# Spreading per-token values over the partitions of a one-core Trainium2 convolution layer: split columns against a rounded identity

## The reference

```
hn = x * rsqrt(mean(x*x) + eps) * norm_g                 # per token
a, b, gate = split(hn @ w_in, 3)                         # w_in 1024 x 3072
u  = a * sigmoid(b)
u  = causal depthwise conv of u, 31 taps, + conv_b
u  = (u - mean(u)) * rsqrt(var(u) + eps) * ln_g + ln_b   # per token
y  = x + (silu(u) * silu(gate)) @ w_out                  # w_out 1024 x 1024
```

## Time and profile before

| | |
|---|---|
| median of 3 runs | 356.37 us (356.23 to 356.69) |
| the profiled execution | 356.49 us, span 354.7 us |
| granted TensorE clock | 1.00 over the whole span |
| PE (matmul) | 349.1 us busy, 98% |
| PEld (weight load) | 288.6 us, 81% |
| DVE (VectorE) | 323.1 us, 91% |
| ACT (ScalarE) | 232.2 us, 65% |
| POOL (GpSimd) | 270.2 us, 76% |
| chain that ended last | PE 82%, DVE 8%, issue 3%, DMA 2% |

### The profile page before, as it was taken

The page is one execution under the profiler, slowest core; times in us unless marked ns, Lnnn a source line. Parts: engine busy times, 40 slices in busy tenths (PEclk is TensorE's granted clock), DMA queues, the critical chain, the costliest instruction groups (busy, mean ns, idle before and its releaser), DMA issues.

```text
span 354.7 us, 4758 instructions
## 1 busy us (share of the span) xinstructions
PE 349.1 (98%) x1564; PEld 288.6 (81%) x1564; DVE 323.1 (91%) x514; ACT 232.2 (65%) x334; POOL 270.2 (76%) x194
## 2 busy tenths in 40 slices
PE   8999999999999999999999999999999999999996
PEld 7878888888888888888888888888788877888886
DVE  4779799999999999989999998997699999999972
ACT  6899684667936870998659777976774872443400
POOL 0129999999999998789999999885698551359240
DMA  7995011211410321404120411341733497046152
GB/s 255 404 412 225 33 61 59 71 50 59 118 61 10 91 80 59 118 2 118 59 60 6 115 59 31 99 109 61 234 121 119 138 416 276 2 136 219 63 206 90
DMA packets 30520, 43.51 MB, mean 123 GB/s; under 512 B 18336, under 2 KB 18848, under 8 KB 30496
## 3 DMA queue, kind: packets, MB, share of 16 engines
q1 hardware_dynamic: 30352, 43.21, 36.7%
q10 hardware_dynamic: 144, 0.00, 0.0%
HBM read 34.82 MB, written 4.19 MB: 110 GB/s over the span
## 4 chain that ended last, share of the span: by engine, by line
PE 82%; DVE 8%; issue 3%; DMA 2%; SPq 2%; ACT 2%; DVEq 0%; ACTq 0%
PE mm L634 63%; PE acc L713 9%; PE mm L713 8%; DMA sgate<-x 2%; DVE nat L1207 2%; DVE x_lo L1243 2%; PE mm L651 2%; SPq L496 1%; DVE sgate L1236 1%; DVE nat L1228 1%; ACT mm L939 1%; DVE sgate L1263 1%; DVE nat L1275 0%; SPq L522 0%; ACT sgate L775 0%
## 5 line engine op out<-in xcount | busy, mean ns | idle before, releaser
L634 PE MATMUL mm<-x_hi,w_hi 128*128 128x512 f32 x352 | 137.4, 390 | 0.0
L634 PE MATMUL mm<-x_hi,w_lo 128*128 128x512 f32 x352 | 137.0, 389 | 0.0
L634 PE MATMUL mm<-x_lo,w_hi 128*128 128x512 f32 x352 | 136.9, 389 | 0.0
L1187 DVE SCALAR_TENSOR_TENSOR acc<-u,chan,acc 128x512 f32<-128x512 f32 x157 | 110.4, 747 | 0.1
L1496 POOL TENSOR_TENSOR pconv<-pconv,prod 128x512 f32<-128x512 f32 x60 | 78.2, 1344 | 1.3 <-ACT prod L870 1.3
L634 PEld LDWEIGHTS mm<-x_hi,w_hi 128*128 128x128 f32 x352 | 66.1, 188 | 13.6
L634 PEld LDWEIGHTS mm<-x_hi,w_lo 128*128 128x128 f32 x352 | 66.1, 188 | 13.7
L634 PEld LDWEIGHTS mm<-x_lo,w_hi 128*128 128x128 f32 x352 | 66.1, 188 | 13.6
L1187 DVE SCALAR_TENSOR_TENSOR acc<-u,w_sum,acc 128x512 f32<-128x512 f32 x90 | 67.2, 746 | 2.4 <-ACT acc L852 2.3
L870 ACT ACTIVATE prod<-u,chan 128x512 f32<-128x512 f32 x69 | 48.0, 716 | 19.9 <-POOL pconv L1496 18.4
L1440 POOL TENSOR_TENSOR w_lo<-raw,w_hi 128x1024 fp32r<-128x1024 f32 (+1 forms) x21 | 50.2, 2390 | 8.8 <-ACT w_hi L819 8.8
(11 more groups left out here) (109 smaller groups left out, 536.2 us busy)
## 6 DMA issues: line engine op xcount, KB each, us to landing
raw<-w_in SPq DMA_DIRECT2D x22, 512.0 KB, 3.4
nat<-x_t SPq DMA_DIRECT2D x16, 256.0 KB, 6.2
sgate<-x SPq DMA_DIRECT2D x8, 512.0 KB, 10.2
raw<-w_out SPq DMA_DIRECT2D x8, 512.0 KB, 3.3
nat<-x SPq DMA_DIRECT2D x8, 512.0 KB, 6.8
y<-nat SPq DMA_DIRECT2D x15, 256.0 KB, 2.2
raw_late<-w_out SPq DMA_DIRECT2D x4, 512.0 KB, 3.8
sig<-w_out SPq DMA_DIRECT2D x4, 512.0 KB, 4.3
```

The costliest lines, as they stand in the source:

```text
L634: ins = nc.tensor.matmul(bank(("unit", m, h)), w[:, m % 3, k, :], xx[:, k, half(h)], start=(k == 0 and i == 0), stop=(k == KC - 1 and i == 2))
L1187: ins = nc.vector.scalar_tensor_tensor(dst, chain_in(j, chain, k), tap(j, chain, k), chain_bank(j, chain), ALU.mult, ALU.add)
```

## The change

All six spreads are done in one way. A column of four per-token values is split into a rounded high part and a rounded low part (fp32r, four numbers per partition each). For each tile, TensorE takes the high column, broadcast to 128 columns, as the stationary operand against a rounded identity of 128 columns, and then the low column in the same way, accumulated. That is 8 fp32r matmuls of 128 columns for each spread, with 8 weight loads. The diagonals of VectorE and of ScalarE and the rounded ones go; a rounded identity is made once by VectorE. The two parts of rms and of the mean are made by VectorE (for rms in `split_rms`, for half 1 ahead of `split_raw(0, 5)` and for half 0 behind the last `make_hn` of half 1; for the mean at the end of `moments`), those of rstd by GpSimd behind the power in `inverse_deviation`. Buffers in SBUF are moved a little.

```diff
-DIAGS_BEFORE = {4: (4, 5, 6), 5: (7,)}
+SPLIT_RMS_BEFORE = 5
...
+            def spread_columns(spread, hi, lo, h):
+                for i in range(TPH):
+                    t = TPH * h + i
+                    nc.tensor.matmul(spread[:, i * P:(i + 1) * P], hi[:, t:t + 1].to_broadcast([P, P]), ident_r[:],
+                                     start=True, stop=False)
+                    ins = nc.tensor.matmul(spread[:, i * P:(i + 1) * P], lo[:, t:t + 1].to_broadcast([P, P]), ident_r[:],
+                                           start=False, stop=True)
+                return ins
             def spread_rms(h):
                 if h == 1:
-                    spread = rms_spread(1).rearrange("p (t q) -> p t q", t=TPH)
-                    pe.wait_ge(ones_r_ready, 1)
-                    pe.wait_ge(diag_hi_ready, TPH)
-                    nc.tensor.matmul(spread, ones_r[:], diags[:, 0, :, :], start=True, stop=False)
-                    pe.wait_ge(diag_lo_ready, TPH)
-                    ins = nc.tensor.matmul(spread, ones_r[:], diags[:, 1, :, :], start=False, stop=True)
-                else:
-                    for i in range(TPH):
-                        pe.wait_ge(diag_ready, i + 1)
-                        ins = nc.tensor.matmul(rms_spread(0)[:, i * P:(i + 1) * P], ones[:], diag(i), start=True, stop=True)
-                ins.then_inc(rms_all_ready, 1)
+                    pe.wait_ge(ident_r_ready, 1)
+                pe.wait_ge(rms_lo_ready, NH - h)
+                spread_columns(rms_spread(h), rms_hi, rms_lo, h).then_inc(rms_all_ready, 1)
...
             def spread_mean(h):
-                pe.wait_ge(mv_ready, TPH * (h + 1))
-                for i in range(TPH):
-                    ins = nc.tensor.matmul(norm_spread(h, 0)[:, i * P:(i + 1) * P],
-                                           mean_var[:, TPH * h + i, 0:1].to_broadcast([P, P]), ident[:],
-                                           start=True, stop=True)
-                ins.then_inc(mean_spread, 1)
+                pe.wait_ge(mean_lo_ready, h + 1)
+                spread_columns(norm_spread(h, 0), mean_hi, mean_lo, h).then_inc(mean_spread, 1)
             def spread_rstd(h):
                 pe.wait_ge(rstd_ready, h + 1)
-                for i in range(TPH):
-                    t = TPH * h + i
-                    ins = nc.tensor.matmul(norm_spread(h, 1)[:, i * P:(i + 1) * P],
-                                           rstd[:, t:t + 1].to_broadcast([P, P]), ident[:], start=True, stop=True)
-                ins.then_inc(rstd_spread, 1)
+                spread_columns(norm_spread(h, 1), rstd_hi, rstd_lo, h).then_inc(rstd_spread, 1)
...
-            for t in range(TPH):
-                rms_diagonal(t)
...
-            nc.vector.tensor_scalar(ones_r[:], ones[:], 1.0, None, ALU.mult).then_inc(ones_r_ready, 1)
+            def split_rms(h):
+                dve.wait_ge(rms_ready, rms_count(TPH * (h + 1) - 1))
+                nc.vector.tensor_scalar(rms_hi[:, tiles_of(h)], rms[:, tiles_of(h)], 1.0, None,
+                                        ALU.mult).then_inc(rms_hi_ready, 1)
+                dve.wait_ge(rms_hi_ready, NH - h)
+                nc.vector.tensor_tensor(rms_lo[:, tiles_of(h)], rms[:, tiles_of(h)], rms_hi[:, tiles_of(h)].bitcast(F32),
+                                        ALU.subtract).then_inc(rms_lo_ready, 1)
...
+                dve.wait_ge(mv_ready, TPH * (h + 1))
+                nc.vector.tensor_scalar(mean_hi[:, tiles_of(h)], means, 1.0, None, ALU.mult).then_inc(mean_hi_ready, 1)
+                dve.wait_ge(mean_hi_ready, h + 1)
+                nc.vector.tensor_tensor(mean_lo[:, tiles_of(h)], means, mean_hi[:, tiles_of(h)].bitcast(F32),
+                                        ALU.subtract).then_inc(mean_lo_ready, 1)
...
-                for t in DIAGS_BEFORE.get(k, ()):
-                    rms_diagonal(t)
+                if k == SPLIT_RMS_BEFORE - 1:
+                    dve.wait_ge(ident_in, 16)
+                    nc.vector.tensor_scalar(ident_r[:], ident[:], 1.0, None, ALU.mult).then_inc(ident_r_ready, 1)
+                if k == SPLIT_RMS_BEFORE:
+                    split_rms(1)
...
+            split_rms(0)
...
-                                        ALU.pow).then_inc(rstd_ready, 1)
+                                        ALU.pow).then_inc(rstd_pow, 1)
+                pool.wait_ge(rstd_pow, h + 1)
+                nc.gpsimd.tensor_scalar(rstd_hi[:, part], rstd[:, part], 1.0, None, ALU.mult).then_inc(rstd_hi_ready, 1)
+                pool.wait_ge(rstd_hi_ready, h + 1)
+                nc.gpsimd.tensor_tensor(rstd_lo[:, part], rstd[:, part], rstd_hi[:, part].bitcast(F32),
+                                        ALU.subtract).then_inc(rstd_ready, 1)
```

More of the change, by code:

```diff
@@ L164, in gated_conv_layer @@
         sig = sb("sig", [P, 2, HALF])
-        sb("gap_before_w", [P, 96])
+        ident_r = sb("ident_r", [P, P], F32R)
+        rms_hi = sb("rms_hi", [P, NT], F32R)
+        rms_lo = sb("rms_lo", [P, NT], F32R)
+        mean_hi = sb("mean_hi", [P, NT], F32R)
+        mean_lo = sb("mean_lo", [P, NT], F32R)
+        rstd_hi = sb("rstd_hi", [P, NT], F32R)
+        rstd_lo = sb("rstd_lo", [P, NT], F32R)
+        sb("gap_before_w", [P, 48])
         first = ExitStack()
@@ L177, in gated_conv_layer @@
             pconv = sb("pconv", [P, 2, HALF], F32, first)
-            ones_r = sb("ones_r", [P, P], F32R, first)
-            diags = sb("diags", [P, 2, TPH, P], F32R, first)
         wb = {}
@@ L200, in gated_conv_layer @@
         ones_ready = sem("ones_ready")
-        ones_r_ready = sem("ones_r_ready")
-        diag_ready = sem("diag_ready")
-        diag_hi_ready = sem("diag_hi_ready")
-        diag_lo_ready = sem("diag_lo_ready")
+        ident_r_ready = sem("ident_r_ready")
+        rms_hi_ready = sem("rms_hi_ready")
+        rms_lo_ready = sem("rms_lo_ready")
+        mean_hi_ready = sem("mean_hi_ready")
+        mean_lo_ready = sem("mean_lo_ready")
+        rstd_hi_ready = sem("rstd_hi_ready")
         rms_all_ready = sem("rms_all_ready")
@@ L241, in gated_conv_layer @@
         veps_ready = sem("veps_ready")
+        rstd_pow = sem("rstd_pow")
         rstd_ready = sem("rstd_ready")
@@ L460, in half, with tiles_of @@
             return slice(h * HALF, (h + 1) * HALF)
-        def diag(i):
-            return sgate[:, i, 0:P]
+        def tiles_of(h):
+            return slice(TPH * h, TPH * (h + 1))
         def words(columns):
@@ L789, in split_first @@
                                      raw[:, m, first_columns(part)], ACT.Copy).then_inc(w_first_hi, 1)
-            def rms_diagonal(t):
-                act.wait_ge(ident_in, 16)
-                act.wait_ge(rms_ready, rms_count(t))
-                nc.scalar.activation(diag(t), ident[:], ACT.Copy, scale=rms[:, t:t + 1]).then_inc(diag_ready, 1)
             def copy_rms(h):
@@ L1075, in _ @@
             nc.vector.memset(ones[:], 1.0).then_inc(ones_ready, 1)
-            dve.wait_ge(ones_ready, 1)
-            nc.vector.tensor_scalar(ones_r[:], ones[:], 1.0, None, ALU.mult).then_inc(ones_r_ready, 1)
             nc.vector.memset(half_neg[:], -0.5).then_inc(exponent_ready, 1)
@@ L1081, in _ @@
             dve.wait_ge(pads_ready, 2)
-            def rms_diagonal(t):
-                dve.wait_ge(ident_in, 16)
-                dve.wait_ge(rms_ready, rms_count(t))
-                i = t - TPH
-                nc.vector.tensor_scalar(diags[:, 0, i, :], ident[:], rms[:, t:t + 1], None,
-                                        ALU.mult).then_inc(diag_hi_ready, 1)
-                dve.wait_ge(diag_hi_ready, i + 1)
-                nc.vector.scalar_tensor_tensor(diags[:, 1, i, :], ident[:], rms[:, t:t + 1],
-                                               diags[:, 0, i, :].bitcast(F32), ALU.mult,
-                                               ALU.subtract).then_inc(diag_lo_ready, 1)
+            def split_rms(h):
[5 more added lines that the diff above has]
+                                        ALU.subtract).then_inc(rms_lo_ready, 1)
             def make_hn(h, k):
@@ L1202, in moments @@
                                       stats[:, t, :, :].rearrange("p g s -> p (g s)")).then_inc(mv_ready, 1)
+                means = mean_var[:, tiles_of(h), 0]
+                dve.wait_ge(mv_ready, TPH * (h + 1))
[3 more added lines that the diff above has]
+                                        ALU.subtract).then_inc(mean_lo_ready, 1)
             def centre(k, h):
```

## The result

The changed kernel takes 359.21 us (median of 4 runs, 359.09 to 359.34) against 356.47 us of the kernel before on the same chip (4 runs, 356.23 to 356.69): ratio 1.0077, 95% interval 1.006 to 1.0094. It is slower by 2.7 us; forecast were 1.1. The profiled execution grew from 356.49 to 359.21 us, its span from 354.7 to 357.1. So 2.4 us of the growth lie inside the span, and 0.3 outside it, between the span and the measured time.

What follows compares the result with a forecast made beforehand. TensorE alone bounds 36.94 to 254.58 us; afterwards VectorE's addition at 293.48 sets the end. The terms -0.03 (head) + 1.16 (rstd pairs on GpSimd) gave +1.1 us, 356.37 to 357.5 us, whole range 356.5 to 360.3 us.

Steps and rivals of the forecast that it cites:

- likeliest case: Whole kernel: the prediction's own sum, +1.1 us to 357.5 us, with its own range 356.9 to 358.4 us, chance 0.60.
- wide price of a narrow matmul: Rival on TensorE: a narrow matmul costs as much as a wide one, 0.227 us; +3.8 us, 360.2 us, chance 0.15.
- The price of a new spread: TensorE, each spread: 8 narrow matmuls at their weight loads' pace, 0.113 us each, 0.90 us a spread.
- rms(1), -0.03 us: Head, spread of rms(1): longer matmuls cost +0.45 us, TensorE's wait of 0.48 us goes; sum -0.03 us.
- rms(0), "Nothing": Spread of rms(0): 0.90 for 0.91 us on TensorE, VectorE's pair inside its idle 2.85 us; no change.
- Mean, 0.40 us a half: VectorE, end of `moments`: two dependent small instructions, 0.40 us a half, 0.80 in all; `centre` about 0.6 us later.
- rstd, 1.16 us on GpSimd: GpSimd behind the power: two instructions, 0.58 us a half; first scale, ScalarE's second SiLU and VectorE's gate 1.16 us later.
- "From 263.92 to 293.48 [...] nothing gives it back": VectorE up to TensorE's last wait: it waits only for ScalarE, which waits for it, so the 1.16 us stay.
- wait of 1.5 us for rstd(0): TensorE: its wait for rstd(0), about 0.93 us, grows by 0.58 to about 1.5 us, taken up by later waits.
- rivals of the matmul's price: TensorE, a narrow matmul at 0.227 us (360.2 us, chance 0.15) or 0.066 us (near 357.0 us, chance 0.08).

Runs made afterwards that it cites:

- e7: Changed kernel with all six spreads as float32 matmuls of the broadcast column, no splits or diagonals: 356.69 us, 1.0006 of the kernel before.
- e9: Changed kernel with rms two words apart and a third VectorE instruction copying rms into PSUM for the rms(0) subtract: 358.48 us, 1.0052 of the kernel before.
- e10: Changed kernel with the rms(0) split made by GpSimd right behind its power, none on VectorE: 358.24 us, 1.0046 of the kernel before.
- e3: Changed kernel with rms(0) spread by float32 matmuls of the broadcast column, without a split: 358.29 us, 1.0056 of the kernel before.
- e1: Changed kernel with the mean's subtract reading a copy of the high part in PSUM: 359.14 us, 1.0081 of the kernel before.
- e2: Changed kernel with the mean's spreads as in the kernel before, float32 without a split: 359.35 us, 1.0083 of the kernel before.
- e5: Changed kernel with rms(0) and both means spread in float32, leaving rms(1) and GpSimd's rstd pairs: 358.45 us, 1.0054 of the kernel before.
- e4: Changed kernel with the rstd spreads as in the kernel before, GpSimd without its pairs: 358.32 us, 1.006 of the kernel before.
- e6: Changed kernel with rms(0) and both rstd spread in float32, leaving rms(1) and the mean's split: 357.19 us, 1.0016 of the kernel before.
- e12: Changed kernel with GpSimd making the rms(0) pair, and its weight subtracts, deviations and scales reordered at 254 us: 358.51 us, 1.0058 of the kernel before.

## Why the prediction was off

The direction was right, and 359.21 lies in the whole range, but outside the 356.9 to 358.4 us of the likeliest case. That the whole range holds it is luck: the range reached so far only for the rival with the wide price of a narrow matmul, and that mechanism fell. Step by step:

- *The price of a new spread*: right. Narrow matmuls are 0.11 us apart, a spread 0.9 us, but for rstd(0) at the lower clock (0.21 and 1.6 us, which reached nothing). e7 adds that float32 spreads cost the same.
- *rms(1), -0.03 us*: right within what can be read; the wait at 23.26 went, and the pair took 0.16 and 0.17 us.
- *rms(0), "Nothing"*: wrong, and this is the step that failed. It took the pair as two short instructions inside VectorE's wait of 2.85 us. The wait ends only when the spread is there, which now needs the pair, so it covers a pair only up to a little over 1 us (e9's three instructions took 1.13 and cost nothing); and the pair was 1.96 us long in place of 0.35, as it had to stand for GpSimd's x_lo group (0.74 and 1.19 us). Price: 1.04 us at the restart of VectorE, carried whole to 254 us. e9 and e10 brought the restart back, and each took 0.7 us off the median span.
- *Mean, 0.40 us a half*: wrong in size for half 0, 2.5 us, by the same mechanism (and by a race that VectorE lost by 0.01 us). `centre` was 3.9 us late (1.04 of it from rms(0)) in place of 0.6. TensorE stood 1.48 us, and its granted clock fell afterwards (it didn't in e3, where it stood 1.58 us): the windows of the changed kernel (busy us of each engine, then the clock, third from last) show 0.74 in 256 to 262 us.

```profile
250.00:256.00 6.00, 5.68 (x26) 4.36 (x24) 3.47 (x10) 4.82 (x8) 3.68 (x2) 1.00 0.66 196
256.00:262.00 6.00, 4.84 (x23) 4.43 (x24) 5.90 (x16) 3.58 (x5) 5.31 (x10) 0.74 0.60 215
```

  None of this reached the end: e1 and e2 undo it, and the time stays.
- *rstd, 1.16 us on GpSimd*: right in size, 1.20 us from first weight subtract to last pair. The way it was to take was only half right. ScalarE's second SiLU does come later, and VectorE stands for it where nothing else has made it late (1.04 us in e5, 0.47 in e10); but in the changed kernel VectorE was late by itself and never stood there. What carries the 1.16 us in every kernel with the pairs is GpSimd's own queue, up to its last pair of scales. In e9 and e10, 1.5 us apart in VectorE's arrival and 0.14 in the start of that pair, the gate is at the same time.
- *"From 263.92 to 293.48 [...] nothing gives it back"*: wrong. It took VectorE's row of four `x_lo` subtracts, 4.57 us, as work; 2.1 us of it is standing for GpSimd. Of VectorE's 3.85 us of delay the shorter meeting took up 1.44.
- *TensorE*: the wait of 1.5 us for rstd(0) that was forecast isn't there; it stood 1.48 us for the mean in its place. What it stands before its last wait costs nothing, as said; that last wait ended at 296.64, forecast near 295.3.
- *Two small slips*: by its own terms the lower bound of the likeliest case is 356.37 - 0.03 + 0.76 = 357.1 us and not 356.9, and twice its price gives 358.7 and not 358.4; 359.21 lies outside either way. And GpSimd's least instruction in the trace of before is a one-element memset of 0.10 us, not 0.19; the pairs took 0.23 and 0.20.

The sum as it should have been: 0.0 (head) + 1.04 (rms(0)) + 1.20 (GpSimd's pairs) + 0.17 (the meeting, 4.87 for 4.70) = 2.41 us, and the span grew by 2.4. The 0.3 us outside the span are in no term of the prediction; with them it is 2.7. The rivals of the matmul's price both fell with the 0.11 us. No rival had a small instruction that stands for another engine, though the 4.57 us of four subtracts whose like take 2.48 elsewhere was in the trace of before.

What stays open: why TensorE's first wait for weights varies from 0 to 1.6 us between runs; what makes the 0.3 us outside the span; and a version faster than both kernels was not found. e7 equals the kernel before.

## What to carry to other kernels

Price a small VectorE instruction by what GpSimd runs at that moment, not by its own 0.16 us: with its operands in SBUF it can last until GpSimd's current instruction ends, and here an operand or a result in PSUM avoided that. Which of the two engines starts first can hang on 0.01 us, so one profile doesn't show what the next run will do. Where a group of instructions takes longer in one place than its like elsewhere, part of it is a wait, and the engine on the other side of that wait may be the one that sets the end. Before one instruction is held back to avoid a meeting, look at which queues wait for its result: ScalarE's and SyncE's made that the dearest experiment here.

## What the runs showed of the hardware

- A subtract of 128x4 with two SBUF inputs took 2.37 us beside a GpSimd instruction of 2.36 us that started within 0.01 us of it, and 0.16 us in the same place with one input in PSUM. In e4 and e10 it took 0.16 us with both inputs in SBUF, and there the two starts are the same in the profile. Where it was held (the changed kernel, e3, e6, e9), GpSimd's start is the same or up to 0.02 us earlier.
- A rounding of 128x4 from SBUF to SBUF, which has one input, is held too: 0.74 us (contiguous, and two words apart), 1.96 us in e12. Into PSUM it took 0.17 us beside the same GpSimd group. The Trainium skill, "VectorE: DVE Perf Modes", section "Why PSUM operands drop a tier", has a reason that agrees with the 0.17 us: the fast mode that works through two ports needs both SBUF read ports, and an operand in PSUM rules it out.
- In twelve profiles GpSimd's two scales and VectorE's four subtracts took 4.66 to 4.87 us from the first scale's start, though VectorE came to them anywhere from 0.2 to 2.4 us behind it (at 2.4 us, in e6, without a meeting).
